# Strassen-type products of a hybrid attention and pooling layer: the rounded operand and its rest as one 512-column moving operand, and the spread of the norms by transposition

## The chip, the cores and the metric

The kernel runs on one core of a Trainium2 chip (trn2). The metric is the device time of one execution in microseconds, as the median of several runs. A core has a tensor engine (PE), a vector engine (DVE), a scalar engine (ACT), GpSimd (POOL) and SyncE (SP), which issues most DMAs. Each engine works through its own queue in order. They meet only at semaphores.

## The reference

One layer on x of 512 tokens x 2048 features, float32:

```python
hn   = RMSNorm(x) * pre_gain
q, k, v, g_a, u_b, g_b = split(hn @ w_in)          # 2048 -> 6 x 1024
z    = q k^T / sqrt(128)                           # 8 heads x 128, strictly causal
A    = sigmoid(z) * prod over s<j<t of (1 - sigmoid(z_tj))
y_a  = (A @ v) * silu(g_a)
y_b  = ((trailing mean of u_b over 2/4/8/16 tokens) - u_b) @ w_pool * pool_scale * silu(g_b)
x    = x + RMSNorm(concat(y_a, y_b) @ w_out) * post_gain
```

## The kernel before

**Arithmetic.** PE multiplies in a rounded 32-bit format (float32r). To keep float32 accuracy each operand is split into a rounded part (hi) and its rest (lo), and each product is three matmuls: hi x hi, hi x lo, lo x hi. They all stand in `three`, lines 1257 to 1259. A weight chunk `raw` of 128 x 1024 gets its `w_hi` on ACT (L470) and its `raw_lo` on DVE (L813).

**Values stage.** It takes 16 steps of K, each with 24 matmuls of 512 columns, and gives v for all tokens and heads in the 8 banks of PSUM. x comes transposed (`mix`); ACT makes `x_hi` (L451), DVE `x_lo` (L805). Beside it the norms are made. ACT squares x by rows (L475), DVE scales the sums (L904), POOL raises them to -1/2 (L1212). The result is one number per token, spread over the partitions; it must come to lie along the free dimension, on all 128 partitions (`rstd_rows`). Before, ACT issues a DMA into DRAM (L533) and another that broadcasts it back (L541). Then DVE multiplies `mix` by gain and `rstd_rows` (`hn_of`, L848) and forms the operands of the next stage.

**Product stage.** The other projections are 40 chunks of 128 output features. Two chunks form a unit, so there are 20 units. A unit is a 2 x 2 block product of Strassen's kind (Winograd's form): K is halved (8 tiles of 128 each) and the tokens are halved (256 each). Seven products replace eight: A11, R1, S2, S4, S3, A12, A22, the moving operands, made once for all units. Each lies in `a_hi` and `a_lo`. A product is 8 K tiles x 3 matmuls of 256 columns; stationary are `w_hi` or `raw_lo`. Products alternate between two PSUM banks, and later ones add onto what earlier ones left. ACT copies products 0, 1, 2 and 6 out (L567, L571, L573, L575), DVE combines products 3, 4 and 5 with these copies (L942, L944, L947). The weight sums that Strassen's form needs are made by DVE (`w_sum`, L828) and by accumulating DMAs of POOL.

Between the products of a unit PE does attention and pooling (`qk`, `suffix_sums`, `weighted_values`, `pool_tiles`), in a written-out order that repeats every five units. The softmax-like work on `tri` (128 x 1280) is on ACT, DVE and POOL.

**Output stage.** mix @ w_out, in 16 chunks of 128 x 2048 weights, split into hi and lo again. The split mix goes to the place of the first four operands in `a_hi` and `a_lo` (`mix_hi_of` L653, `mix_lo_of` L1042), three of the four weight slots to that of the last three (`o_hi_of` L665, `o_lo_of` L1051); the fourth is `o_hi3`/`o_lo3`.

What PE waits for before product p of unit u is in `product`: w_lo of this product; the copy or the combination of product p-2, whose bank it takes. ACT's w_hi of a product waits until the one three before is done, so both run at most two products ahead.

## Time and profile before

| | |
|---|---|
| median of 3 runs (lowest, highest) | 754.19 us (754.01, 757.17) |
| profiled execution: own time, span | 756.16 us, 754.4 us |
| PE busy, instructions | 736.1 us, 4912 matmuls |
| DVE busy, instructions | 481.5 us, 572 |
| ACT busy, instructions | 389.9 us, 530 |
| granted TensorE clock | 0.998 of full speed |
| HBM | 156 GB/s over the span |

The span goes from the first to the last instruction. Roughly, 0 to 100 us is the values stage, 101 to 567 the products with attention and pooling between them, 567 to 747 the output stage, and then the last rows are stored. In a row of the timeline the number in front is the start, the second the duration of one instruction (for x2 or x4, of all together); in brackets stands the idle time before it and what released it. Durations of matmuls overlap, so the pace is read from the starts.

### The profile page before, as it was taken

The numbers are of one execution on the slowest core, as the hardware profiler recorded it, in microseconds if no ns is written. First come the engines' busy times: TensorE is split into PE (matmuls) and PEld (weight loads), VectorE is DVE, ScalarE is ACT, GpSimd is POOL, SyncE is SP. The second block draws the span as 40 slices with busy tenths as digits, with TensorE's granted clock in tenths as the row PEclk, the third lists the DMA queues.
The fourth block names the chain that finished last, engine by engine and source line by source line (L and its number), as shares of the span: only waits on it lengthen the run. The fifth ranks groups of instructions, "written<-read, shape, count | busy, mean of one in ns | idle before, by whom it ended". The sixth has DMA issues, their size and how long they took to land.

```text
span 754.4 us, 11839 instructions
## 1 busy us (share of the span) xinstructions
PE 736.1 (98%) x4912; PEld 679.6 (90%) x4912; DVE 481.5 (64%) x572; ACT 389.9 (52%) x530; POOL 62.4 (8%) x85
## 2 busy tenths in 40 slices
PE   7999989999999999999999999999999999999996
PEld 5778879999999999999999999999998888888884
DVE  3379976767677767875786966776688532142333
ACT  4645466646656646665655566655569332132200
POOL 0000000110020110011100021020010000000000
PEclk9999999999999999999999999999999999999999
DMA  8944435666645756666555566556645613152242
GB/s 316 368 151 126 141 81 147 166 164 188 165 116 164 194 144 171 154 163 168 162 146 158 168 165 172 151 121 180 175 150 214 223 41 132 51 168 90 78 140 111
DMA packets 37060, 118.48 MB, mean 157 GB/s; under 512 B 4752, under 2 KB 5776, under 8 KB 36368
## 3 DMA queue, kind: packets, MB, share of 16 engines
q1 hardware_dynamic: 30288, 96.49, 37.1%
q0 software_dynamic: 5760, 20.97, 16.7%
q8 instruction: 39, 0.64, 0.3%
q10 hardware_dynamic: 960, 0.27, 0.2%
q14 instruction: 13, 0.11, 0.0%
HBM read 113.52 MB, written 4.20 MB: 156 GB/s over the span
## 4 chain that ended last, share of the span: by engine, by line
PE 83%; DVE 7%; DMA 4%; issue 3%; ACT 2%; SPq 1%; DVEq 0%; POOLq 0%; POOL 0%; ACTq 0%
PE ps L1257 27%; PE ps L1258 27%; PE ps L1259 27%; DMA mix<-xT 2%; PE ps L1348 1%; DVE mix L848 1%; DVE raw_lo L813 1%; PE ps L1346 1%; DMA rstd_rows<-rstd_dram 1%; DVE a_lo L881 1%; DVE a_lo L878 1%; DMA rstd_dram<-rstd_by_four 1%; ACT w_hi L470 1%; SPq L367 1%; DVE sum L853 0%
## 5 line engine op out<-in xcount | busy, mean ns | idle before, releaser
L1257 PE MATMUL ps<-a_hi,w_hi 128*128 128x256 f32 x1120 | 318.2, 284 | 3.5 <-ACT p_neg L571 1.3
L1258 PE MATMUL ps<-a_lo,w_hi 128*128 128x256 f32 x1120 | 316.9, 283 | 0.0
L1259 PE MATMUL ps<-a_hi,raw_lo 128*128 128x256 f32 x1120 | 316.8, 283 | 0.0
L813 DVE TENSOR_TENSOR raw_lo<-raw,w_hi 128x1024 fp32r<-128x1024 f32 x155 | 189.3, 1223 | 58.7 <-ACT w_hi L470 58.0
L1257 PEld LDWEIGHTS ps<-a_hi,w_hi 128*128 128x128 f32 x1120 | 214.8, 192 | 4.6 <-issue 3.0
L1258 PEld LDWEIGHTS ps<-a_lo,w_hi 128*128 128x128 f32 x1120 | 214.8, 192 | 0.4
L1259 PEld LDWEIGHTS ps<-a_hi,raw_lo 128*128 128x128 f32 x1120 | 214.8, 192 | 0.0
L470 ACT ACTIVATE w_hi<-raw 128x1024 fp32r<-128x1024 f32 x155 | 163.5, 1055 | 75.7 <-PE ps L1259 71.5
L1257 PE MATMUL ps<-a_hi 128*128 128x512 f32 x192 | 74.9, 390 | 0.0
L1258 PE MATMUL ps<-a_lo,a_hi 128*128 128x512 f32 x192 | 74.8, 390 | 0.0
L1259 PE MATMUL ps<-a_hi,a_lo 128*128 128x512 f32 x192 | 74.7, 389 | 0.0
L1228 POOL DMA_DIRECT2D raw<-w_heads x40 | 34.9, 871 | 322.4 <-DMA raw<-w_heads 286.1
L828 DVE TENSOR_TENSOR raw<-raw 128x1024 f32<-128x1024 f32 x40 | 48.8, 1220 | 10.5 <-DMA raw<-w_heads 9.5
L1051 DVE TENSOR_TENSOR a_lo<-raw,a_hi 128x1024 fp32r<-128x1024 f32 x24 | 28.5, 1229 | 39.1 <-ACT a_hi L665 39.1
L1257 PE MATMUL ps<-w_hi,x_hi 128*128 128x512 f32 x120 | 47.6, 397 | 2.4 <-DVE raw_lo L813 2.4
L665 ACT ACTIVATE a_hi<-raw 128x1024 fp32r<-128x1024 f32 x24 | 24.1, 1051 | 45.2 <-PE ps L1259 45.2
L1258 PE MATMUL ps<-raw_lo,x_hi 128*128 128x512 f32 x120 | 47.4, 395 | 0.0
L1259 PE MATMUL ps<-w_hi,x_lo 128*128 128x512 f32 x120 | 47.4, 395 | 0.0
L1259 PEld LDWEIGHTS ps<-a_hi,a_lo 128*128 128x128 f32 x192 | 36.1, 188 | 7.5
L1257 PEld LDWEIGHTS ps<-a_hi 128*128 128x128 f32 x192 | 36.1, 188 | 7.5
L1258 PEld LDWEIGHTS ps<-a_lo,a_hi 128*128 128x128 f32 x192 | 36.1, 188 | 7.4
L1218 POOL TENSOR_SCALAR_AFFINE_SELECT tri<-tri 128x256 f32<-128x256 f32 x32 | 24.0, 772 | 165.3 <-ACT tri L604 84.9
(135 smaller groups left out, 869.1 us busy)
## 6 DMA issues: line engine op xcount, KB each, us to landing
raw<-w_heads SPq DMA_DIRECT2D x100, 512.0 KB, 4.2
raw<-w_heads POOLq DMA_DIRECT2D x40, 512.0 KB, 6.4
raw<-w_out SPq DMA_DIRECT2D x32, 512.0 KB, 4.9
raw<-w_v SPq DMA_DIRECT2D x15, 512.0 KB, 11.7
mix<-xT SPq DMA_DIRECT2D x16, 256.0 KB, 10.5
x_rows<-x SPq DMA_DIRECT2D x4, 1024.0 KB, 13.3
raw<-x SPq DMA_DIRECT2D x8, 512.0 KB, 4.4
out<-mix SPq DMA_DIRECT2D x6, 512.0 KB, 2.7
```

What stands on the lines that cost most here:

```text
L367: sp.dma_start(raw_slot(raw, slot).rearrange("p (g c) -> p g c", g=2), v_weights(i)).then_inc(raw_loaded[slot], 16)
L470: act.activation(hi_slot(g), raw_slot(raw, slot), ACT.Copy).then_inc(w_hi_done, 1)
L665: act.activation(out_weights(a_hi, o_hi3, n % OUT_SLOTS)[:, b * QUARTER:(b + 1) * QUARTER], raw_slot(raw, half_slot(j)), ACT.Copy).then_in ...
L813: dve.tensor_tensor(raw_slot(raw_lo, slot), raw_slot(raw, slot), hi_slot(g).bitcast(F32), ALU.subtract).then_inc(w_split, 1)
L828: dve.tensor_tensor(raw_slot(raw, ROLE[u][p]), raw_slot(raw, ROLE[u][a]), raw_slot(raw, ROLE[u][b]), ALU.add).then_inc(w_summed, 1)
L848: dve.scalar_tensor_tensor(mix_tile(k), mix_tile(k), pre_gain_col[:, k:k + 1], rstd_rows[:, :], ALU.mult, ALU.mult).then_inc(hn_done, 1)
L1051: dve.tensor_tensor(out_weights(a_lo, o_lo3, n % OUT_SLOTS)[:, cols], raw_slot(raw, half_slot(j)), out_weights(a_hi, o_hi3, n % OUT_SLOTS) ...
L1218: pool.affine_select(out=sq, in_=sq, compare_op=ALU.is_gt, fill=0.0, base=0, pattern=[[0, 2], [1, P]], channel_multiplier=-1).then_inc(don ...
L1228: pool.dma_start(raw_slot(raw, slot), w_heads[unit_chunks(u)[1]][:, a:a + QUARTER], accum_op=ALU.add).then_inc(done, 16)
L1257: pe.matmul(dst, sta[0], mov[0], start=first, stop=False, skip_group_check=True)
L1258: pe.matmul(dst, sta[0], mov[1], start=False, stop=False, skip_group_check=True)
L1259: return pe.matmul(dst, sta[1], mov[0], start=False, stop=last, skip_group_check=True)
```

## The change

**Operands.** `a_hi` and `a_lo` become one tensor `a_ops`. A K tile of an operand is now 512 columns wide, 256 of hi and beside them 256 of lo. In a product, `w_hi` is multiplied with all 512 in one matmul, and `raw_lo` with the 256 of hi, into the second half of the bank. So a bank holds two partial results of 256 columns, which somebody must add.

**Drains.** ACT's copies of products 0, 1 and 2 and DVE's combinations of 3, 4 and 5 are 512 wide now. After each combination DVE folds: it adds the two halves (256 columns, out of SBUF). For product 6 ACT copies one half and DVE adds the other, a new instruction that stands at the start of the next unit in DVE's queue. PE waits for combinations, not for folds.

**Norms.** x is loaded by rows in natural order; the last of the four loads goes behind x and w_v of step 4, and the last square behind x_hi and w_hi of step 4. POOL's result is transposed by DVE in blocks of 32 x 32, and 16 small copies (8 on DVE, 8 on ACT) spread it over the partitions. The DMAs through DRAM are gone, and `rstd_col` needs none either.

**Output stage.** It computes the same; only the places of its operands within `a_ops` change.

```diff
             for i in (1, 2, 3): ...
-            square_of(3)
             x_hi_of(4)
             w_hi_of(4)
+            square_of(3)
             for i in range(2, V_STEPS):
-                if i == 3:
-                    act.wait_ge(rstd_ready, 1)
-                    act.dma_start(rstd_dram.rearrange("(p s) -> p s", s=TT),
-                                  rstd_by_four[:, :]).then_inc(rstd_sent, 16)
+                if i == 2:
+                    act.wait_ge(rstd_turned, 1)
+                    for to in (2, 3):
+                        for q in range(QUADRANTS):
+                            act.activation(rstd_part(to, q), turned_part(q), ACT.Copy).then_inc(rstd_spread, 1)
...
+            x_lo_of(4)
+            w_lo_of(4)
             dve.wait_ge(squared, TT)
             dve.tensor_scalar(ms_col[:, :], ss_col[:, :], 1.0 / D, EPS, ALU.mult,
                               ALU.add).then_inc(ms_ready, 1)
-            x_lo_of(4)
-            w_lo_of(4)
+            dve.wait_ge(rstd_ready, 1)
+            dve.transpose(sum1[:, 0:P].rearrange("p (s t) -> p s t", s=TT),
+                          rstd_col[:, :].unsqueeze(2).to_broadcast([P, TT, QUADRANT])).then_inc(rstd_turned, 1)
+            dve.wait_ge(rstd_turned, 1)
+            for to in (0, 1):
+                for q in range(QUADRANTS):
+                    dve.tensor_copy(rstd_part(to, q), turned_part(q)).then_inc(rstd_spread, 1)
...
             def combine(u, p):
...
                 if p == 3:
...
-                    dve.tensor_tensor(n2[:, 0:HALF], p2_neg[:, :], src, ALU.subtract).then_inc(combined, 1)
+                    dve.tensor_tensor(n2, p2_copy(u), src, ALU.subtract).then_inc(combined, 1)
+                    dve.wait_ge(combined, 4 * u + 1)
+                    dve.tensor_tensor(n2[:, 0:HALF], n2[:, 0:HALF], n2[:, HALF:SEQ],
+                                      ALU.add).then_inc(folded, 1)
...
-                    dve.tensor_tensor(n1[:, 0:HALF], p0_copy(u), src, ALU.add).then_inc(combined, 1)
+                    dve.wait_ge(copied, 4 * u + 4)
+                    dve.tensor_tensor(n1[:, HALF:SEQ], src[:, 0:HALF], n1[:, HALF:SEQ],
+                                      ALU.add).then_inc(combined, 1)
...
                 for p in range(PRODUCTS):
                     if p in (4, 5, 6):
                         combine(u, p - 1)
+                    if p == 0 and u > 0:
+                        combine(u - 1, 6)
...
             def product(u, p):
...
                 for k in range(KH):
-                    a = p * OPERAND + k * HALF
-                    mm = three(dst, both((hi, lo), k * P, (k + 1) * P), both((a_hi, a_lo), a, a + HALF),
-                               k == 0 and p in (0, 1, 5), k == KH - 1)
+                    a = p * OPERAND + k * SEQ
+                    w = slice(k * P, (k + 1) * P)
+                    pe.matmul(dst, hi[:, w], a_ops[:, a:a + SEQ], start=k == 0 and p in (0, 1, 5),
+                              stop=False, skip_group_check=True)
+                    mm = pe.matmul(dst[:, HALF:SEQ], lo[:, w], a_ops[:, a:a + HALF], start=False,
+                                   stop=k == KH - 1, skip_group_check=True)
```

On DVE in the values stage, from the scaling of the sums (`ms_col`) to the first `hn_of`, before:

```order
L904 TENSOR_SCALAR ms_col<-ss_col 128x4
L805 SCALAR_TENSOR_TENSOR x_lo<-mix,pre_gain_col,x_hi 128x512
L813 TENSOR_TENSOR raw_lo<-raw,w_hi 128x1024
L805 SCALAR_TENSOR_TENSOR x_lo<-mix,pre_gain_col,x_hi 128x512 x2
L813 TENSOR_TENSOR raw_lo<-raw,w_hi 128x1024
L805 SCALAR_TENSOR_TENSOR x_lo<-mix,pre_gain_col,x_hi 128x512
L813 TENSOR_TENSOR raw_lo<-raw,w_hi 128x1024
L848 SCALAR_TENSOR_TENSOR mix<-mix,pre_gain_col,rstd_rows 128x512 x4
```

The same place on DVE now:

```order
L822 SCALAR_TENSOR_TENSOR x_lo<-mix,pre_gain_col,x_hi 128x512
L830 TENSOR_TENSOR raw_lo<-raw,w_hi 128x1024
L924 TENSOR_SCALAR ms_col<-ss_col 128x4
L927 STREAM_TRANSPOSE sum<-rstd_col 128x128
L932 COPY rstd_rows<-sum 32x4x32 x8
L822 SCALAR_TENSOR_TENSOR x_lo<-mix,pre_gain_col,x_hi 128x512 x2
L830 TENSOR_TENSOR raw_lo<-raw,w_hi 128x1024
L822 SCALAR_TENSOR_TENSOR x_lo<-mix,pre_gain_col,x_hi 128x512
L830 TENSOR_TENSOR raw_lo<-raw,w_hi 128x1024
L867 SCALAR_TENSOR_TENSOR mix<-mix,pre_gain_col,rstd_rows 128x512 x4
```

x_lo and w_lo of step 4 stand ahead of the norms now, and nine instructions of the spread stand ahead of those of step 5.

On DVE in the last unit, from the combination of product 3 (`mix<-p_neg,ps`) over the softplus on `tri` to `gate_logsig` behind the loop, before:

```order
L942 TENSOR_TENSOR mix<-p_neg,ps 128x256
L961 SCALAR_TENSOR_TENSOR tri<-ps,tri 128x1280
L813 TENSOR_TENSOR raw_lo<-raw,w_hi 128x1024
L944 TENSOR_TENSOR mix<-p_neg,ps 128x256
L1051 TENSOR_TENSOR a_lo<-raw,a_hi 128x1024 x2
L947 TENSOR_TENSOR mix<-mix,ps 128x256
L966 TENSOR_TENSOR tri_lo<-tri,tri_hi 128x1280
L987 SCALAR_TENSOR_TENSOR gate_work<-mix,gate_work 128x512
```

The same place on DVE now:

```order
L968 TENSOR_TENSOR mix<-mix,ps 128x512
L970 TENSOR_TENSOR mix<-mix 128x256
L1001 SCALAR_TENSOR_TENSOR tri<-ps,tri 128x1280
L830 TENSOR_TENSOR raw_lo<-raw,w_hi 128x1024
L973 TENSOR_TENSOR p_neg<-p_neg,ps 128x512
L976 TENSOR_TENSOR mix<-p_neg 128x256
L1090 TENSOR_TENSOR a_ops<-raw,a_ops 128x1024 x2
L980 TENSOR_TENSOR mix<-mix,ps 128x512
L982 TENSOR_TENSOR mix<-mix 128x256
L1006 TENSOR_TENSOR tri_lo<-tri,tri_hi 128x1280
L986 TENSOR_TENSOR mix<-ps,mix 128x256
L1027 SCALAR_TENSOR_TENSOR gate_work<-mix,gate_work 128x512
```

Three folds came in behind the three combinations, and the combination of product 6 (L986) ahead of `gate_logsig`. In the other units it stands at the same point relative to the loop, ahead of the first `w_sum` of the next unit.

## Rows read from the trace of the kernel before

**Rows 1.** The page: busy us (share) xinstructions by engine; GB/s in 40 slices.
```profile
PE 736.1 (98%) x4912; PEld 679.6 (90%) x4912; DVE 481.5 (64%) x572; ACT 389.9 (52%) x530; POOL 62.4 (8%) x85
...
GB/s 316 368 151 126 141 81 147 166 164 188 165 116 164 194 144 171 154 163 168 162 146 158 168 165 172 151 121 180 175 150 214 223 41 132 51 168 90 78 140 111
```

**Rows 2.** Waits of PE: line, releaser: us in total, times, longest us.
```profile
PE ps L1257 <- DVE raw_lo L813: 2.4, 2, 1.8
PE ps L1257 <- ACT p_neg L571: 1.3, 1, 1.3
PE ps L1257 <- ACT mix L514: 1.1, 1, 1.1
PE ps L1257 <- ACT work L567: 1.1, 1, 1.1
```

**Rows 3.** Page, part 5: line, operation, shapes, xcount | busy, mean ns | idle.
```profile
L1257 PE MATMUL ps<-a_hi,w_hi 128*128 128x256 f32 x1120 | 318.2, 284 | 3.5 <-ACT p_neg L571 1.3
```

**Rows 4.** Timeline, PE in unit 8: start us, us, line, operation, xcount.
```profile
300.00 0.28 PE L1257 MATMUL ps<-a_hi,w_hi 128*128 128x256 f32 x1
...
302.88 0.28 PE L1257 MATMUL ps<-a_hi,w_hi 128*128 128x256 f32 x1
```

**Rows 5.** Timeline, PE in the output stage.
```profile
615.50 0.39 PE L1257 MATMUL ps<-a_hi 128*128 128x512 f32 x1
...
648.16 0.40 PE L1257 MATMUL ps<-o_hi,a_hi 128*128 128x512 f32 x1
...
659.13 0.40 PE L1259 MATMUL ps<-o_hi,a_lo 128*128 128x512 f32 x1
```

**Rows 6.** Timeline, POOL, ACT and DVE in the values stage.
```profile
28.15 1.02 POOL L1212 TENSOR_TENSOR rstd_by_four<-ms_col,neg_half 128x4 f32<-128x4 f32 x1 [26.36 <-DVE ms_col L904]
...
46.65 0.71 ACT L451 ACTIVATE x_hi<-mix,pre_gain_col 128x512 fp32r<-128x512 f32 x1
47.26 1.04 ACT L470 ACTIVATE w_hi<-raw 128x1024 fp32r<-128x1024 f32 x1
...
42.61 2.74 DVE L848 SCALAR_TENSOR_TENSOR mix<-mix,pre_gain_col,rstd_rows 128x512 f32<-128x512 f32 x4 [2.65 <-DMA rstd_rows<-rstd_dram]
...
48.34 1.23 DVE L813 TENSOR_TENSOR raw_lo<-raw,w_hi 128x1024 fp32r<-128x1024 f32 x1 [0.19 <-ACT w_hi L470]
```

**Rows 7.** Timeline, ACT and PE in unit 0.
```profile
111.28 1.26 ACT L514 ACTIVATE mix<-ps,rstd_col 128x512 f32<-128x512 f32 x2 [1.95 <-DVE a_lo L878]
...
112.97 0.36 PE L1257 MATMUL ps<-a_hi,w_hi 128*128 128x256 f32 x1 [1.33 <-ACT p_neg L571]
```

**Rows 8.** Groups by form on DVE: a 512-column instruction that reads PSUM.
```profile
L982 DVE TENSOR_TENSOR mix<-ps,mix 128x512 f32<-128x512 f32 x8 | 5.5, 691 | 0.7
```

**Rows 9.** Stretch 400:500: us, busy us (xinstructions) by engine, clock, DMA.
```profile
400.00:500.00 100.00, 100.00 (x809) 98.94 (x808) 74.69 (x84) 62.38 (x84) 12.02 (x14) 1.00 0.61 161
```

**Rows 10.** Timeline, DVE and PE at weighted_values of head 2.
```profile
274.59 1.49 DVE L971 TENSOR_TENSOR tri_lo<-tri,tri_hi 128x1280 fp32r<-128x1280 f32 x1
...
277.62 0.39 PE L1257 MATMUL ps<-tri_hi,v_hi 128*128 128x512 f32 x1
```

**Rows 11.** Timeline, DVE, ACT and PE in the last unit and after.
```profile
560.24 0.41 DVE L942 TENSOR_TENSOR mix<-p_neg,ps 128x256 f32<-128x256 f32 x1
...
561.97 1.21 DVE L813 TENSOR_TENSOR raw_lo<-raw,w_hi 128x1024 fp32r<-128x1024 f32 x1
...
568.10 0.69 DVE L987 SCALAR_TENSOR_TENSOR gate_work<-mix,gate_work 128x512 f32<-128x512 f32 x1 [0.36 <-ACT gate_work L631]
...
571.33 2.49 DVE L1042 TENSOR_TENSOR a_lo<-mix,a_hi 128x512 fp32r<-128x512 f32 x4
...
570.92 0.36 ACT L575 ACTIVATE mix<-ps 128x256 f32<-128x256 f32 x1
...
564.00 0.28 PE L1257 MATMUL ps<-a_hi,w_hi 128*128 128x256 f32 x1
...
575.17 0.39 PE L1257 MATMUL ps<-a_hi 128*128 128x512 f32 x1
```

More of the change, by code:

```diff
@@ L377, in _ @@
                 load_x_rows(i - 1)
+            load_x(4)
+            load_v(4)
             load_x_rows(3)
-            for i in (4, 5, 6):
+            for i in (5, 6):
                 load_x(i)
@@ L490, in a_hi_of @@
             def a_hi_of(q, op):
-                dst = operand(a_hi, op, q)
+                dst = operand(0, op, q)
                 if op in (A11, A12, A22):
@@ L495, in a_hi_of @@
                     half, tok = {A11: (0, 0), A12: (1, 0), A22: (1, 1)}[op]
-                    act.activation(split3(dst), pairs(mix, q, half, tok), ACT.Copy).then_inc(a_hi_done, 1)
+                    act.activation(dst, pairs(mix, q, half, tok), ACT.Copy).then_inc(a_hi_done, 1)
                     return
@@ L652, in mix_hi_of @@
                     act.wait_ge(pool_free, k - HEADS + 1)
[L653 removed]
+                act.activation(mix_part(k, 0), mix_tile(k), ACT.Copy).then_inc(mix_hi_done, 1)
             def o_hi_of(n):
@@ L1050, in o_lo_of @@
                     dve.wait_ge(o_hi_done, j + 1)
-                    dve.tensor_tensor(out_weights(a_lo, o_lo3, n % OUT_SLOTS)[:, cols],
+                    dve.tensor_tensor(out_weights(1, n % OUT_SLOTS)[:, cols],
                                       raw_slot(raw, half_slot(j)),
-                                      out_weights(a_hi, o_hi3, n % OUT_SLOTS)[:, cols].bitcast(F32),
+                                      out_weights(0, n % OUT_SLOTS)[:, cols].bitcast(F32),
                                       ALU.subtract).then_inc(o_split, 1)
@@ L1396, in _ @@
                             pool_tiles(2 * i + 1)
-            acts = (a_hi, a_lo)
             def rows_tile(dc, s, c):
                 slot = (KK * dc + c) % OUT_SLOTS
-                hi = out_weights(a_hi, o_hi3, slot)
-                lo = out_weights(a_lo, o_lo3, slot)
+                hi, lo = out_weights(0, slot), out_weights(1, slot)
                 for k in range(KC):
-                    a = (OUT_KK[c] * KC + k) * SEQ + s * P
-                    mm = three(rows_bank(dc, s), both(acts, a, a + P),
+                    tile = OUT_KK[c] * KC + k
+                    mm = three(rows_bank(dc, s), both((mix_part(tile, 0), mix_part(tile, 1)), s * P, (s + 1) * P),
                                both((hi, lo), k * BANK, (k + 1) * BANK),
```

149 lines of the change are left out of this document (81 added, 68 removed).

## The prediction

> **What bounds the kernel now.** I read the busy table first. The tensor engine (PE) is busy for 98% of the span, the vector engine (DVE) for 64%, the scalar engine (ACT) for 52% [rows 1]. The waits of PE come next: besides the first load there are five, worth 5.9 us of idle time, and they all lie in the first 115 us [rows 2]. From there to the end PE never waits. So time can only come from what PE does per instruction, from those early waits, or be lost where another engine becomes late.
>
> A busy row says nothing about pace, since matmuls overlap. The groups by form give the count: 1120 K tiles in the 140 products, three matmuls of 256 columns each [rows 3]. The starts give the pace. Between the two starts in [rows 4] lie 24 matmuls: 2.88 us / 24 = 120 ns, so 360 ns for a K tile, 403 us in all. That is over half of the span. The output stage shows 512 columns with new weights each time: 144 steps in 32.66 us = 226.8 ns where the moving operand lies in a_hi or a_lo, 47 steps in 10.97 us = 233.4 ns where it lies in o_hi3 or o_lo3 [rows 5].
>
> **The product's K tile.** Three matmuls of 256 columns become one of 512 (w_hi against a_hi and a_lo side by side) and one of 256 (raw_lo against a_hi). Columns stay at 768, weight loads go from three to two. Were time only columns, 512 would cost 2 x 120 = 240 ns and nothing would be won. The rows show 226.8 to 233.4, so about 7 to 13 ns belong to the instruction and not to its columns. The new pair then costs 226.8 + 120 = 347 ns or 233.4 + 120 = 353 ns. The moving operand of the products lies in a_ops, where a_hi was, which is the case of the first number; the stationary one is w_hi, which no 512 row has in that place. I take 348.5, nearer the first. Saving: 11.5 ns x 1120 = 12.9 us; ends 7.3 and 14.6 us, and 0 if the alternation of sizes costs what the merging gives.
>
> Here the Trainium skill speaks against the change (TensorE: Matmul & The Clock Gate, section Back-to-back issue gap): a warm matmul is spaced by its columns at 2.4 GHz plus about 2.5 ns, whatever its size. An estimate by that page is 2.5 x 1120 = 2.8 us saved. The trace does not agree with its sizes: 256 columns take 120 ns and not 109, 512 take 227 to 233 and not 216, at a granted clock of full speed.
>
> **The spread of the norms.** Now POOL's power ends at 28.15 + 1.02 = 29.17 us, and the first scaling of x by rstd_rows starts at 42.61 on DVE, because two DMAs through DRAM lie between [rows 6]. From there DVE works almost without a pause, and w_lo of value step 7 is ready only at 48.34 + 1.23 = 49.6; PE waits 1.8 us for it [rows 2, 6]. Its other wait on raw_lo, 0.6 us, is for step 4. A value step is 24 matmuls of about 233 ns, 5.6 us. So step 7 was due at 47.8, and steps 4 to 6 fill the time from 31.0 on. After the change, step by step:
> - The loads of x and w_v for step 4 pass the last megabyte of x_rows. DVE has w_lo of step 4 earlier and the 0.6 us wait goes: step 4 starts at 30.4.
> - 0.75 MB now go ahead of the last of x_rows, 2.0 us at 368 GB/s [rows 1]. The last square comes later by that and the power ends near 31.2.
> - DVE transposes (one instruction of 128 columns, then 8 copies of 128), ACT makes 8 more. No row has this shape. The nearest is a 256-column DVE instruction of 0.41 us [rows 11]; a shorter one should last less, and a queue of them starts faster than they last, so I take 0.2 us each, ends 0.1 and 0.41. Both engines are done near 33.3 (ends 32.5 and 35).
> - ACT's copies now stand ahead of x_hi(5), x_hi(6) and w_hi(5) in its queue. x_hi holds it for 0.61 us, w_hi lasts 1.04, w_lo after it 1.23 [rows 6]: w_lo of step 5 is ready near 36.9, and PE wants it at 36.0. A new wait of 0.9 us.
> - w_lo of step 6 follows within DVE's next 1.8 us, so the scaling starts near 38.6, 4 us earlier. w_lo of step 7 comes near 45.6 against a demand at 48.1, so the 1.8 us wait goes.
> Net so far: 0.6 + 1.8 - 0.9 = 1.5 us.
>
> DVE stays busy from here until the last a_lo, so its 4 us lead goes on to the first products. Three waits stand there: 1.1 for the value drain, 1.1 for the copy of product 0, 1.3 for the copy of product 1 [rows 2, 7]. The last is a chain: a_lo on DVE, two drains on ACT from 111.28, the copy, PE at 112.97 [rows 7]. With DVE 4 us earlier, that product starts near 109.4. The copies of 512 columns add 0.25 us to this chain. Product 4 starts about 3.5 us earlier than now; this 3.5 us contains the 1.5 above. Ends: 1 us (the small copies cost double and delay step 5 by 3 us) and 4.5 us.
>
> **The wider drains.** A DVE instruction on 512 columns out of PSUM takes 691 ns [rows 8], on 256 columns 0.41 us; ACT pays 0.36 us for 256 [rows 11] and 1.26 us for two drains of 512 [rows 7]. Per unit of seven products ACT gets three copies 0.25 us longer. DVE gets three combinations 0.27 us longer, three folds of 256 columns (0.35 us each) and a fourth combination of 0.35 us that waits for ACT's copy: some 2.3 us per 20 us. DVE has 75 us of work in 100 us there [rows 9], so it rises to about 87% and still fits. What hides it is PE's work on the other bank. The tightest recurring place that the longer drains touch is weighted_values: DVE's weights_lo ends at 274.59 + 1.49 = 276.08, PE needs it at 277.62 [rows 10], slack 1.5 us. ACT's wider copy takes 0.25 of it, faster products 0.2, about 1 us stays. A combination is now done one product less 0.7 us before PE needs its bank, 2.2 us; 0.3 to 0.5 of that goes. So I cost all of it at nothing in units 0 to 18. If that cover were gone, each unit would lose what DVE is behind.
>
> **The last unit.** Here DVE has the output operands to split as well, and does not idle. The combination of product 3 starts at 560.24 only, w_lo of product 6 ends at 561.97 + 1.21 = 563.2, and PE starts product 6 at 564.00 [rows 11]. After the change ACT's copies push by 0.25, combination and fold add 0.6, and the next combination (on which product 6 waits too) 0.3: ready at 564.8, wanted at 563.65. PE loses 1.2 us. The same once more at the handoff to the output stage: 0.4 us. Then the new combination of product 6 stands in DVE's queue ahead of gate_logsig. It waits for ACT's copy, which ends now at 571.3 (570.92 + 0.36) and then near 572.2, since the longer DVE chain delays POOL's mask and so ACT. Behind it are queued, as now from 568.10 to 571.33 + 2.49 = 573.82, 5.7 us of work ending with the mix operands that PE needs at 575.17 [rows 11]. From 572.6 that gives 578.0; PE, delayed by the above, wants it at 576.4. Wait 1.6 us. Sum 3.2 us lost; ends 0.5 and 5.
>
> **The sum**, against the profiled execution (span 754.4, own time 756.16): - 12.9 - 3.5 + 3.2 = - 13.2, span 741.2, own time 743.0. The median of before is 754.19, 2 us under that execution; the same step gives 741.0. I forecast 741.
>
> **Rivals.**
> - The pair costs what three cost (360 ns): the alternation breaks the overlap of loads and matmuls. For it: no row alternates 512 and 256. Against: the 226.8. Then 754.2 - 3.5 + 3.2 = 754. Chance 0.07.
> - Only a small part per instruction is saved. As a mechanism: the extra over columns in [rows 4, 5] (13 to 20 ns per matmul) goes with the columns read, and 2 to 3 ns with the instruction. Then 3 us are won and the time is 751. This is the rule of the Trainium skill's page named above. Chance 0.04.
> - Slower: DVE becomes the bound in the product loop. Place: w_lo in the iterations that now also hold combination and fold. It decides from the point at which DVE is behind by more than its slack of about 1.5 us; then each of 19 units loses about one w_lo (1.13 us), 21.5 us in all: 741 + 21.5 = 762. Against it speak the 75% of [rows 9]. Chance 0.05.
> - Better: the pair at 347 ns, early waits all gone (4.5), handoff at 0.5: 754.2 - 14.6 - 4.5 + 0.5 = 735.6. Chance 0.12.
> - The rest is worse than thought (pair 353, startup 1, handoff 5): 754.2 - 7.3 - 1 + 5 = 751, half of it under 750. Chance 0.08.
> - The forecast, 736 to 747: 0.64.
>
> **How the numbers follow.** What a measurement of this kernel can tell from no change is about 0.5%, 3.8 us: faster is under 750.4. Forecast, better and half of the last case give 0.80, and of the cases near 751 and of the slower one a part would still end under it: 0.86. Same 0.09, slower 0.05. The range 735 to 750 leaves out the two no-gain rivals and the slower one.
>
> **What would show it.** Starts of the two matmuls of a K tile: 227 to 233 ns and then 120 ns apart (right), 240 and 120 (wrong). The scaling of x starting at 38 to 39 us, a wait of about 1 us for w_lo of step 5. Product 4 starting near 112. No PE wait from there to the last unit; if there are waits on DVE there, the slower rival is at work. In the last unit waits on DVE of about 3 us in sum. A loop without waits and a time above 750 would say that the pair costs more than 357 ns.

## The result and the profile after

The changed kernel takes 749.34 us (median of 6 runs, 749.08 to 750.37), the kernel before 754.11 us on the same chip. The ratio is 0.994, 95% interval 0.993 to 0.995: 4.8 us won. The forecast was 741 us, 13.2 us won. The sign was right, the time lies in the range of 735 to 750, 0.7 us from its end, and the gain was overrated by a factor of nearly three. Of all executions used below one, the profiled one of e9_moved_64, ran at a granted clock of 0.825 and took 821.9 us; no time or row is taken from it.

The page of the changed kernel, busy time and the two groups of the product stage; they answer to [rows 1, 3].

```profile
span 747.4 us, 9753 instructions
...
PE 726.2 (97%) x3792; PEld 618.4 (83%) x3792; DVE 527.9 (71%) x661; ACT 406.0 (54%) x538; POOL 62.8 (8%) x85
...
L1361 PE MATMUL ps<-a_ops,w_hi 128*128 128x512 f32 x1120 | 397.9, 399 | 3.6 <-ACT p_neg L584 1.6
L1363 PE MATMUL ps<-a_ops,raw_lo 128*128 128x256 f32 x1120 | 314.2, 281 | 0.0
```

1120 matmuls of 512 and 1120 of 256 columns stand where 3360 of 256 stood. DVE rose from 481.5 to 527.9 us, 71%, and is still far from being the bound.

All waits of PE in the changed kernel, in the columns of [rows 2]:

```profile
PE ps L1316 <- ACT w_hi L538: 6.3, 1, 6.3
PE ps L1299 <- DVE raw_lo L830: 2.1, 2, 1.8
PE ps L1361 <- ACT p_neg L584: 1.6, 1, 1.6
PE ps L1361 <- ACT work L580: 1.4, 1, 1.4
PE ps L1299 <- DVE a_ops L1082: 1.1, 1, 1.1
PE ps L1361 <- DVE p_neg L973: 0.5, 1, 0.5
PE ps L1299 <- DVE mix L980: 0.3, 1, 0.3
```

The first is the first load. The next three lie before 111 us, the last three in the last unit and at the handoff to the output stage. Between 111 and 553 us PE waits for nobody.

A second execution of the kernel before was profiled too (`e1_before_again`), and it is the fairer basis, since it is nearer its median. The span by stages, in us, from the starts of PE's instructions (units 1 to 18 go from the first matmul of unit 1 to the first of unit 19; the recorded expectations call the same stretch units 1 to 19):

| | before, again (e1) | changed | difference |
|---|---|---|---|
| start to the first product | 100.54 | 98.67 | -1.87 |
| unit 0 | 23.12 | 23.22 | +0.10 |
| units 1 to 18 | 418.60 | 411.24 | -7.36 |
| unit 19 | 23.45 | 24.65 | +1.20 |
| output stage | 180.06 | 181.50 | +1.44 |
| from the start of the last matmul to the end | 7.47 | 8.12 | +0.65 |
| span | 753.2 | 747.4 | -5.8 |

The table says where the forecast went: units 1 to 18 gave 7.4 us where their share of the 12.9 was 11.6. The time up to unit 1 fell by 1.8 us, 0.4 of it by the pairs of unit 0, so 1.4 stand against a forecast of 3.5. The end took about what was forecast.

### The profile page after: what moved, and what is told of

Same layout as the page of the kernel before. It is cut to its first block, busy times and chain, and to the rows that moved or that the text cites. A ratio compares the mean times of both kernels' runs of the same rounds, so it can differ in the third digit from the quotient of the medians.

```text
span 747.4 us, 9753 instructions
## 1 busy us (share of the span) xinstructions
PE 726.2 (97%) x3792; PEld 618.4 (83%) x3792; DVE 527.9 (71%) x661; ACT 406.0 (54%) x538; POOL 62.8 (8%) x85
## 4 chain that ended last, share of the span: by engine, by line
PE 79%; DVE 9%; ACT 4%; issue 3%; DMA 2%; SPq 1%; POOL 0%; DVEq 0%; POOLq 0%; ACTq 0%
PE ps L1361 33%; PE ps L1363 17%; PE ps L1301 9%; PE ps L1300 9%; PE ps L1299 9%; DMA x_rows<-x 2%; DVE raw_lo L830 2%; DVE mix L867 1%; PE ps L1391 1%; PE ps L1389 1%; ACT w_hi L486 1%; DVE a_ops L899 1%; DVE a_ops L897 1%; DVE a_ops L1082 1%; SPq L381 0%
## 5 line engine op out<-in xcount | busy, mean ns | idle before, releaser
L1361 PE MATMUL ps<-a_ops,w_hi 128*128 128x512 f32 x1120 | 397.9, 399 | 3.6 <-ACT p_neg L584 1.6
L1363 PE MATMUL ps<-a_ops,raw_lo 128*128 128x256 f32 x1120 | 314.2, 281 | 0.0
L1361 PEld LDWEIGHTS ps<-a_ops,w_hi 128*128 128x128 f32 x1120 | 210.5, 188 | 55.8 <-DVE raw_lo L830 2.5
L1363 PEld LDWEIGHTS ps<-a_ops,raw_lo 128*128 128x128 f32 x1120 | 211.5, 189 | 0.3
L1299 PE MATMUL ps<-a_ops 128*128 128x512 f32 x192 | 75.0, 391 | 1.4 <-DVE a_ops L1082 1.1
L1300 PE MATMUL ps<-a_ops 128*128 128x512 f32 x192 | 74.8, 390 | 0.0
L1301 PE MATMUL ps<-a_ops 128*128 128x512 f32 x192 | 74.7, 389 | 0.0
L1090 DVE TENSOR_TENSOR a_ops<-raw,a_ops 128x1024 fp32r<-128x1024 f32 x24 | 28.3, 1219 | 37.8 <-ACT a_ops L682 37.8
L682 ACT ACTIVATE a_ops<-raw 128x1024 fp32r<-128x1024 f32 x24 | 24.0, 1050 | 43.9 <-PE ps L1301 42.8
L1299 PEld LDWEIGHTS ps<-a_ops 128*128 128x128 f32 x192 | 36.0, 188 | 9.5 <-issue 2.1
L1301 PEld LDWEIGHTS ps<-a_ops 128*128 128x128 f32 x192 | 36.0, 188 | 7.6
L1300 PEld LDWEIGHTS ps<-a_ops 128*128 128x128 f32 x192 | 36.0, 188 | 7.5
L1206 DVE TENSOR_TENSOR mix<-ps,post_gain_rows 128x512 f32<-128x512 f32 x16 | 11.0, 689 | 40.9 <-ACT gate_work L797 28.2
L797 ACT ACTIVATE gate_work<-ps 128x512 f32<-128x512 f32 x8 | 4.8, 598 | 49.1 <-PE ps L1301 49.1
```

The source lines that it names most:

```text
L682: act.activation(out_weights(0, n % OUT_SLOTS)[:, b * QUARTER:(b + 1) * QUARTER], raw_slot(raw, half_slot(j)), ACT.Copy).then_inc(o_hi_don ...
L1090: dve.tensor_tensor(out_weights(1, n % OUT_SLOTS)[:, cols], raw_slot(raw, half_slot(j)), out_weights(0, n % OUT_SLOTS)[:, cols].bitcast(F3 ...
L1299: pe.matmul(dst, sta[0], mov[0], start=first, stop=False, skip_group_check=True)
L1300: pe.matmul(dst, sta[0], mov[1], start=False, stop=False, skip_group_check=True)
L1301: return pe.matmul(dst, sta[1], mov[0], start=False, stop=last, skip_group_check=True)
L1361: pe.matmul(dst, hi[:, w], a_ops[:, a:a + SEQ], start=k == 0 and p in (0, 1, 5), stop=False, skip_group_check=True)
```

## The experiments

Three explanations were open at the outset: the pair is dearer than forecast in itself, or the small shift of the tiles that comes with the norms' edit makes it dearer, or the two edits get in each other's way at the start. The recorded expectations name theories A, B and so on anew for each run. Four kernels take the change apart.

### The parts alone

`e1_before_again` is the kernel before, unchanged.

> The kernel before, unchanged, for a second profile. The first profiled execution took 756.16 us against a median of 754.1. Theory A (the 2 us are a slow start of that one execution): the span is near 752.4, unit 0 ends about 2 us earlier than in the first profile, everything after it has the same length. Theory B (they lie elsewhere): the starts up to unit 1 (124.56 us) agree within 0.3 us.

Measured: 754.98 us, span 753.2, one run. PE waits for raw_lo once, for 1.2 us, and not twice, for 2.4 us in all [rows 2]. Unit 1 starts at 123.66 us, 0.9 us earlier, and units 1 to 18 take 418.60 us in both. So part of what theory A supposed is there, and 1.2 us of the execution on which the prediction's sum rests were waits at the start that another execution does not have.

`e2_pairs_only` is the changed kernel with the old norms:

```diff
+        rstd_by_four = sb("rstd_by_four", [P, TT])
...
-                    act.wait_ge(rstd_turned, 1)
-                    for to in (2, 3): ...                  # the copies
+                    act.dma_start(rstd_dram..., rstd_by_four[:, :])
```

> The change without its norms: pair of 512 and 256 columns, wide drains and folds, but the spread of the norms through DRAM as before. From the trace after: pair 353.9 instead of 360 ns, 0.41 us per unit, 8.2 us for 20 units, less 2.7 us of waits in the last unit. Theory A (the norms bring almost nothing): 749 to 750, a gain of 4.5 to 5.5. Theory B (the norms bring the 2.5 us that the two profiles show): 751 to 752, a gain of 2 to 3.

Measured: 748.5 us (747.89 to 750.51), ratio 0.9917 (0.990 to 0.993). That is better than both theories had it, and less than the changed kernel takes. Units 1 to 18 take 408.33 us, 2.9 us less than with both edits, though the products are the same instructions on operands at the same places. What lies elsewhere are the tiles behind `rstd_by_four`, those of attention and pooling among them.

`e3_norms_only` is the kernel before with the new norms, tiles kept in place:

```diff
-        rstd_by_four = sb("rstd_by_four", [P, TT])
+        sb("same_place", [P, TT])
```

> The norms by transposition alone, products as before; x_hi and its neighbours stay at the addresses of before. Theory A (before's profile was a slow start): gain 0 to 1 us, 753 to 754. Theory B: gain 2.5 us, 751.5. In both the first scaling of x starts near 39.7 us.

Measured: 752.19 us (751.11 to 752.73), ratio 0.9965 (0.995 to 0.998), between the two theories; units 1 to 18 in 418.60 us as before. The profiled execution is the fastest of the six. In it the first scaling of x starts at 37.86 us and not near 39.7, PE has no wait for w_lo, and unit 1 starts at 119.79 us, 3.9 us earlier than in e1. The last rows of x set this: the last square, on ACT, waits for their DMA and starts here at 26.25 us, in the changed kernel at 28.13.

```profile
26.25 1.92 ACT L483 ACTIVATE x_rows<-x_rows 128x2048 f32<-128x2048 f32 x1 [0.97 <-DMA x_rows<-x]
```

```profile
28.13 1.92 ACT L491 ACTIVATE x_rows<-x_rows 128x2048 f32<-128x2048 f32 x1 [1.37 <-DMA x_rows<-x]
```

So one profile tells what the norms win at the start only to within a microsecond or two; the medians say 2.2 us.

`e4_aligned_only` is the kernel before with a small unused tile that takes 32 bytes per partition, after which x_hi, tri, q, k and o_hi3 lie at multiples of 128 and not at 96 modulo 128. (Places are worked out from the order and sizes of the tiles in the kernel, each rounded up to 32 bytes; the traces do not print them.)

```diff
         rstd_by_four = sb("rstd_by_four", [P, TT])
+        sb("align_pad", [P, TT])
```

> The kernel before with 32 bytes of padding, which puts x_hi, x_lo, o_hi3 and what follows at multiples of 64 bytes, as the changed kernel does by dropping rstd_by_four. Theory A (the faster value steps after, 5.49 instead of 5.60 us, come from the address): value steps take 5.49 us here too. The time: since DVE's chain sets the start of products 2 and 3, PE's 1.5 us turn into longer waits there and the time is within 0.3 us of before. Rival: the steps keep 5.60 us and the faster ones came from something else in the change; or the 1.5 us show in full, 752.6.

Measured: 753.06 us (751.91 to 754.22), ratio 0.9977 (0.997 to 0.999). The output stage takes 178.58 and not 180.06 us: with o_hi3 as the moving operand it now runs at 226.5 ns a matmul and not 233.4 [rows 5]. A step of the values stage takes 5.44 us and not 5.60, but waits at the start take that back: the first product starts at 100.47 us, in e1 at 100.54. Units 1 to 18 take 418.46 us, in e1 418.60: the old products hardly change with these places.

So the pairs are worth 5.8 us, the norms 2.2, the places alone 1.3. The first two should give 8 together; the changed kernel gives 4.8. The change does one thing that neither e2 nor e3 does: without `rstd_by_four` everything behind it moves by 32 bytes.

### The places of the tiles

`e5_shift32` gives the 32 bytes back and `e6_shift64` twice as many; `e7_narrow_first` exchanges the two matmuls of a K tile.

```diff
         rstd_col = sb("rstd_col", [P, TT])
+        sb("pad", [P, 8])        # e5; 16 in e6
```

```diff
-                    pe.matmul(dst, hi[:, w], a_ops[:, a:a + SEQ], start=..., stop=False)
-                    mm = pe.matmul(dst[:, HALF:SEQ], lo[:, w], a_ops[:, a:a + HALF], ...)
+                    pe.matmul(dst[:, HALF:SEQ], lo[:, w], a_ops[:, a:a + HALF], start=..., stop=False)
+                    mm = pe.matmul(dst, hi[:, w], a_ops[:, a:a + SEQ], ...)
```

> The changed kernel with 32 unused bytes per partition ahead of ss_col, so that everything behind them (x_hi, x_lo, tri_hi, tri_lo, q, k, v_hi, work, gate_work, p1_neg) lies where it lay before and in the run with the pairs alone: at 32 modulo 64. a_ops, w_hi, raw, raw_lo do not move, and the instructions are the same. In the changed kernel a product of 8 K tiles takes 2.70 to 2.75 us nearly everywhere (pair 353.5 ns); in the pairs alone about 60% of the products take 2.66 us (pair 347 ns). Theory A (the place of the other tiles decides in which of two paces the products run): units 1 to 19 take 408.3 us in place of 411.2, the short pace shows in units 2, 3 and 5 to 8 as in the pairs alone, time 749.3 - 2.9 = 746.4. Rival B (the norms' edit is to blame, or which pace comes is chance from build to build): units 1 to 19 stay at 411 us, time 749.3. Rival C (the values stage loses what it had gained by the old places, 16 x 0.1 us): the loop gains 2.9 and 1.6 is lost, 748.0.

> The changed kernel with 64 unused bytes at the same place, so everything behind them stays at a multiple of 64 and moves from 64 to 0 modulo 128. Theory A with only 64 as its rule: loop as in the changed kernel, units 1 to 19 411.2 us, time 749.3. Theory A with 128 as its rule: o_hi3 as moving operand of the output stage paces 226.5 ns as in the aligned kernel before (o_hi3 at 0 modulo 128) and not 233.5 as in the changed one (64 modulo 128), which gives 1.3 us in the output stage, 748.0, and the loop may change its pace too. Rival B (chance): anything from 746 to 749.5 with no pattern by unit.

> The changed kernel with the two matmuls of a K tile exchanged: first raw_lo x 256 columns, then w_hi x 512. The bank, the drains and the sums are the same. If each matmul has a price of its own (512: 236, 256: 118), nothing changes: 749.3, the pair at 353 to 354 ns. If the long pace comes from which load stands behind which matmul, the pair changes: 347 ns would give units 1 to 19 in 405.5 us and 743.5; 360 ns would give 757.

Measured. The kernel before, run beside the three new ones, took 753.86 us. A product counts as short when its pairs, without the first, which other work ahead of it can stretch, are under 350 ns apart in the mean; no product lies between 347.8 and 352:

| | us | ratio | units 1 to 18 | products at the short pace | output stage |
|---|---|---|---|---|---|
| changed kernel | 749.34 | 0.994 (0.993 to 0.995) | 411.24 | 13 of 140 | 181.50 |
| pairs only | 748.5 | 0.992 (0.990 to 0.993) | 408.33 | 80 | 181.16 |
| e5_shift32 | 746.3 | 0.990 (0.988 to 0.991) | 408.17 | 82 | 181.49 |
| e6_shift64 | 746.3 | 0.990 (0.988 to 0.991) | 408.92 | 67 | 180.06 |
| e7_narrow_first | 747.39 | 0.991 (0.989 to 0.993) | 408.38 | 77 | 181.53 |

e5 comes out as its theory A to a tenth of a microsecond: with the tiles back at their places, 32 unused bytes win 3 us. In units 1 to 18 it has the short pace in the very 78 products in which the pairs alone have it, and e8 below, a third kernel with these places, has it there too. The sum of the parts holds again (5.8 + 2.2 = 8.0 against 7.6). That the norms' edit itself harms the pairs is refuted, and so is chance from build to build. Rival C is refuted too: the steps of the values stage do return from 5.49 to 5.60 us and the first product starts 1.5 us later than in the changed kernel, but PE's wait for the copy of product 0 shrinks from 1.4 to 0.2 us, and unit 1 starts only 0.4 us later.

In e6 theory A with 64 as its rule is refuted, since the loop is not at 411.2 us. With 128 as its rule it is right for the output stage, below, but the time is 746.3 and not 748.0, since the loop took a third pattern. In e7 none of the three times came: the pairs keep their two paces, in other products. So the places do not decide alone which pace comes; the order of the two matmuls does too.

What "pace" means is seen in the starts of the matmuls. PE in the changed kernel, near 300 us:

```profile
300.22 0.40 PE L1361 MATMUL ps<-a_ops,w_hi 128*128 128x512 f32 x1
300.45 0.28 PE L1363 MATMUL ps<-a_ops,raw_lo 128*128 128x256 f32 x1
300.57 0.40 PE L1361 MATMUL ps<-a_ops,w_hi 128*128 128x512 f32 x1
...
302.34 0.40 PE L1361 MATMUL ps<-a_ops,w_hi 128*128 128x512 f32 x1
```

From 300.22 to 302.34 are six pairs, 353 ns each. Within three pairs the 512 takes 232, 241 and 236 ns, over and over. And PE in e5_shift32, near 250 us:

```profile
249.81 0.39 PE L1362 MATMUL ps<-a_ops,w_hi 128*128 128x512 f32 x1
250.04 0.28 PE L1364 MATMUL ps<-a_ops,raw_lo 128*128 128x256 f32 x1
250.16 0.39 PE L1362 MATMUL ps<-a_ops,w_hi 128*128 128x512 f32 x1
...
251.54 0.39 PE L1362 MATMUL ps<-a_ops,w_hi 128*128 128x512 f32 x1
```

Five pairs in 1.73 us, 346 ns: 230 + 117 each time. (In 12 of the 13 short products of the changed kernel and 43 of the 67 of e6 a second form with the same mean stands, 231 + 113 and 233 + 117 in turn.) Behind the first pair a product is kept at one pace, and so are the next products until attention or pooling work, or a wait, comes between; behind it the pace may be the other. The pattern repeats with the period of five units. In e6 the output stage shows the other effect of places: with o_hi3, the moving operand, at 0 modulo 128 a matmul takes 226.6 ns, at 64 (changed kernel) and 96 (before, e5) 233.5. The values stage shows a third: there only the stationary operands, x_hi and x_lo, change their places with these edits, and yet a step takes 5.44 us at 0 modulo 128 (e4, e6, e10, e12), 5.49 at 64 (changed, e7) and 5.60 at 96 (all others read here).

### The order of work at both ends

`e8_moved_work` is e5 with work moved in three places. At the start:

```diff
-                if i == 2:
+                if i == 3:
                     act.wait_ge(rstd_turned, 1)
                     for to in (2, 3): ...       # now behind x_hi_of(i + 3) and w_hi_of(i + 2)
```

At the end:

```diff
             h = HEADS - 1
-            combine(LAST_UNIT, 6)
             gate_logsig_of(h, 0)
             o_lo_of(1)
+            combine(LAST_UNIT, 6)
```

and, third, in the last unit wp_lo goes behind w_lo. `e9_moved_64` has 64 bytes of padding, `e10_narrow_moved_64` the 256 columns first as well.

> As e5_shift32, with two instructions orders mended. At the start ACT's 8 small copies stand behind w_hi of step 5 and not ahead of x_hi of step 5: PE's wait of 1.8 us for w_lo of step 5 goes, the first scaling of x starts at about 38.0 us (39.7 in the changed kernel). At the end DVE's new combination of product 6 stands behind gate_logsig and the split of the second output chunk, and in the last unit wp_lo behind w_lo. If the waits of PE there (0.31 + 0.68 + 0.47 + 1.28 = 2.7 us) come from this order, they go, and with the start 4.4 us are won against e5_shift32: 742.0. Rival: DVE has no room in the last unit, whatever the order; the waits move and only the 1.7 us of the start are won: 744.7.

> As e8_moved_work, with 64 unused bytes and not 32, so that the tiles behind them lie at 0 modulo 128. If the places act alike with and without the moved work: output stage 1.4 us shorter (o_hi3 as moving operand 226.5 ns and not 233.5), units 1 to 19 in 408.9 us and not 408.2, in sum 742.3 - 1.4 + 0.7 = 741.6. Rival: the loop's pace comes out at random again (408.2 to 411.3), 741 to 744.

> As e9_moved_64, with the 256-column matmul first in each K tile. In e7_narrow_first this exchange gave 408.4 us for units 1 to 19 at places where the other order took 411.2, with the same two paces of 347 and 353.5 ns, only entered at other units. If the exchange only changes in which units the short pace is entered, the loop here lies between 405.5 (all short) and 411.5 (all long) and the time between 738.5 and 744.5; I expect 408.5 and 741.2. If the exchange favours the short pace as such, it is 406 or less, and under 739.

Measured: e8 742.27 us (741.85 to 743.09), ratio 0.984 (0.983 to 0.986); e9 741.6 (741.04 to 742.06), ratio 0.983 (0.981 to 0.984); e10 741.42 (740.82 to 743.24), ratio 0.983 (0.981 to 0.985), with 85 products at the short pace, units 1 to 18 in 408.60 and the output stage in 178.64 us. All three came within 0.3 us of what was expected, and beat the changed kernel by 7 to 8 us. Whether the stages of e9 did what was expected of them no trace shows.

The start in the changed kernel: POOL's power, DVE's transposition and copies, ACT's copies and what is queued behind them, PE's wait for w_lo of step 5, the scaling of x.

```profile
30.42 1.02 POOL L1254 TENSOR_TENSOR rstd_col<-ms_col,neg_half 128x4 f32<-128x4 f32 x1 [28.63 <-DVE ms_col L924]
```

```profile
31.47 0.31 DVE L927 STREAM_TRANSPOSE sum<-rstd_col 128x128 f32<-128x128 f32 x1 [1.14 <-POOL rstd_col L1254]
31.82 1.96 DVE L932 COPY rstd_rows<-sum 32x128 f32<-32x128 f32 x8
...
36.79 1.23 DVE L830 TENSOR_TENSOR raw_lo<-raw,w_hi 128x1024 fp32r<-128x1024 f32 x1
...
39.73 2.73 DVE L867 SCALAR_TENSOR_TENSOR mix<-mix,pre_gain_col,rstd_rows 128x512 f32<-128x512 f32 x4
```

```profile
31.82 2.63 ACT L553 ACTIVATE rstd_rows<-sum 32x128 f32<-32x128 f32 x8 [1.68 <-DVE sum L927]
34.48 1.34 ACT L467 ACTIVATE x_hi<-mix,pre_gain_col 128x512 fp32r<-128x512 f32 x2
35.72 1.04 ACT L486 ACTIVATE w_hi<-raw 128x1024 fp32r<-128x1024 f32 x1
```

```profile
38.16 0.47 PE L1299 MATMUL ps<-w_hi,x_hi 128*128 128x512 f32 x1 [1.84 <-DVE raw_lo L830]
```

Eight copies take DVE 1.96 us (245 ns each) and ACT 2.63 us (329 ns each). ACT waits 1.68 us for the transposition first, with x_hi of step 5 queued behind; w_lo of step 5 is ready at 36.79 + 1.23 = 38.02 and PE loses 1.84 us. In e8 the same places are:

```profile
30.21 1.50 ACT L468 ACTIVATE x_hi<-mix,pre_gain_col 128x512 fp32r<-128x512 f32 x2
31.62 1.04 ACT L487 ACTIVATE w_hi<-raw 128x1024 fp32r<-128x1024 f32 x1
32.69 2.63 ACT L558 ACTIVATE rstd_rows<-sum 32x128 f32<-32x128 f32 x8
```

```profile
35.31 1.22 DVE L831 TENSOR_TENSOR raw_lo<-raw,w_hi 128x1024 fp32r<-128x1024 f32 x1
...
38.25 2.73 DVE L868 SCALAR_TENSOR_TENSOR mix<-mix,pre_gain_col,rstd_rows 128x512 f32<-128x512 f32 x4
```

x_hi and w_hi fill the time in which ACT had waited. The scaling starts at 38.25 (in e5 at 40.09, with the last square within 0.2 us of the same start), and PE's wait for raw_lo, 2.25 us in e5, shrinks to 0.2 us.

The end, DVE in the changed kernel:

```profile
547.36 0.43 DVE L1068 TENSOR_TENSOR wp_lo<-wp_raw,wp_hi 128x256 fp32r<-128x256 f32 x1 [3.13 <-ACT wp_hi L661]
547.70 1.22 DVE L830 TENSOR_TENSOR raw_lo<-raw,w_hi 128x1024 fp32r<-128x1024 f32 x1
...
552.50 1.22 DVE L830 TENSOR_TENSOR raw_lo<-raw,w_hi 128x1024 fp32r<-128x1024 f32 x1
553.63 0.68 DVE L973 TENSOR_TENSOR p_neg<-p_neg,ps 128x512 f32<-128x512 f32 x1
...
561.15 0.42 DVE L986 TENSOR_TENSOR mix<-ps,mix 128x256 f32<-128x256 f32 x1 [1.66 <-ACT mix L591]
561.49 0.68 DVE L1027 SCALAR_TENSOR_TENSOR gate_work<-mix,gate_work 128x512 f32<-128x512 f32 x1
...
564.36 2.90 DVE L1082 TENSOR_TENSOR a_ops<-mix,a_ops 128x512 fp32r<-128x512 f32 x4
```

and PE there:

```profile
554.46 0.47 PE L1361 MATMUL ps<-a_ops,w_hi 128*128 128x512 f32 x1 [0.52 <-DVE p_neg L973]
557.78 0.47 PE L1299 MATMUL ps<-a_ops 128*128 128x512 f32 x1 [0.31 <-DVE mix L980]
567.41 0.47 PE L1299 MATMUL ps<-a_ops 128*128 128x512 f32 x1 [1.12 <-DVE a_ops L1082]
```

wp_lo waits 3.13 us for ACT with the next w_lo behind it, and DVE is late from there on. The new combination (L986) waits 1.66 us for ACT's copy at 560.34, with gate_logsig, o_lo and the mix operands behind it, and PE waits 1.12 us for these. In e8:

```profile
541.35 1.22 DVE L831 TENSOR_TENSOR raw_lo<-raw,w_hi 128x1024 fp32r<-128x1024 f32 x1 [1.70 <-ACT w_hi L487]
542.82 0.43 DVE L1069 TENSOR_TENSOR wp_lo<-wp_raw,wp_hi 128x256 fp32r<-128x256 f32 x1 [0.24 <-ACT wp_hi L662]
...
556.61 0.41 DVE L987 TENSOR_TENSOR mix<-ps,mix 128x256 f32<-128x256 f32 x1
556.95 2.48 DVE L1083 TENSOR_TENSOR a_ops<-mix,a_ops 128x512 fp32r<-128x512 f32 x4
```

Now w_lo stands ahead of wp_lo and starts 12.8 us after the unit's first product (528.6) and not 14.6 (533.1), the combination finds its copy ready with gate_logsig and o_lo done before it, the mix operands start 28.4 us into the unit and not 31.2, and of PE's waits at the end only 0.3 us is left: unit 19 takes 23.53 us and the output stage 180.15, together 2.8 us less than in e5. The rival (DVE has no room there) is refuted. The two moves at the end were made together, and what each is worth is not shown.

### What switches the pace

`e11_extra_columns` and `e13_wide_switched` (both from e8) and `e12_narrow_switched` (from e10) put one useless matmul ahead of some products; in e11:

```diff
                 dst = product_bank(g)
+                extra = EXTRA.get((u, p), 0)
+                if extra:
+                    pe.matmul(dst[:, 0:extra], hi[:, 0:P], a_ops[:, p * OPERAND:p * OPERAND + extra],
+                              start=True, stop=False, skip_group_check=True)
```

> e8_moved_work with one useless matmul of N columns ahead of eight products (its sums are cleared by the product's first matmul, start=True): ahead of product 5 of units 3, 8, 13, 18 with N = 128, 136, 144, 152, and ahead of product 1 of units 4, 9, 14, 19 with N = 160, 168, 176, 184. It shifts the moment at which the product starts by 3.3 ns from one N to the next. In e8_moved_work all eight products and those behind them run at the long pace (353.5 ns a pair). Theory phase: which pace comes is decided by the moment of the start relative to something that ticks, so at some N the product behind runs at 347 ns and keeps it to the end of the unit, at other N it doesn't. Rival position: the pace hangs on where the instructions lie in PE's queue or on what stands ahead of them; then all eight act alike, all long or all short. Time: 742.3 + 8 x 0.065 = 742.8, less 0.05 us for each product that turns short.

> e10_narrow_moved_64 with one useless matmul of 128 columns ahead of product 0 of unit 1 and product 1 of units 5, 10 and 15 (cleared by the product's first matmul). In e10 these four stand at the start of runs of 8, 14, 14 and 14 products at the long pace (353.5 ns a pair, 236 + 118). Theory switch: one more matmul there turns them to the short pace, for at least the products up to the next attention work; if it holds through, 50 products x 8 x 6.5 ns = 2.6 us are won and 4 x 0.115 paid: units 1 to 19 in 406.3 and not 408.6, time 739.2. Rival (chance of the place): products behind it stay at the long pace, time 741.4 + 0.5 = 741.9.

> e8_moved_work with one useless matmul of 128 columns ahead of product 5 of units 3, 8, 13 and 18 alone. In e11 products 5 and 6 and product 0 of the next unit turned to the short pace behind it, and then a second one turned product 1 back. Theory switch: without the second, product 1 of units 4, 9, 14, 19 stays at the short pace too, and what follows depends on the pooling work behind it. Gain at least 4 x (4 x 8 x 6.5 ns - 0.115 us) = 0.4 us, at most 4 x (10 x 8 x 6.5 ns - 0.115) = 1.6 us: 740.7 to 741.9. Rival: 742.3 or more.

e11 took 743.0 us, one run. PE in e11 around the extra matmul ahead of product 5 of unit 3, which stood in a run at the long pace:

```profile
181.75 0.22 PE L1365 MATMUL ps<-a_ops,w_hi 128*128 128x128 f32 x1
181.81 0.45 PE L1370 MATMUL ps<-a_ops,w_hi 128*128 128x512 f32 x1
182.09 0.28 PE L1372 MATMUL ps<-a_ops,raw_lo 128*128 128x256 f32 x1
182.21 0.39 PE L1370 MATMUL ps<-a_ops,w_hi 128*128 128x512 f32 x1
182.44 0.28 PE L1372 MATMUL ps<-a_ops,raw_lo 128*128 128x256 f32 x1
```

From the extra matmul to the start of the 256 are 0.34 us, and then the short pace holds: 0.23 and 0.12. So at all four places with 128 to 152 columns. At the four others, with 160 to 184 columns, the run ahead was at the short pace (an effect of the first four), and behind the extra matmul it was at the long one. The width had no part in it: extra matmul and 512 together take 341 to 346 ns for every width from 128 to 184; what a narrower one saves, the 512 behind it takes longer. Neither theory had this right. The shift of 3.3 ns that "phase" needed never reached the product, so that theory wasn't tested; "position" asked for one answer at all eight places, and they gave two.

In e12 the extra matmul switched unit 1 from long to short, where it stood right between products, and at units 5, 10 and 15, where it stood behind attention work, it did nothing: still 236 ns. Behind unit 1 the rest of unit 2 and the first three products of unit 3, short in e10, came out long. The time is 741.76 us (741.11 to 742.83), and units 1 to 18 take 409.70 against 408.60: the forecast of 739.2 was wrong. The extra matmuls take some 0.5 us of it and a wait for q_lo in unit 4, which e10 does not have, 0.8. e13 behaved as forecast for the products behind (products 5 and 6 and five of the next unit at the short pace), but measured 741.75 us (741.08 to 743.0) against 742.27: half a microsecond, not told apart from nothing. Units 1 to 18 took 408.30 us against 408.17, though 103 and not 78 of their products are short, which is worth 25 x 52 ns = 1.3 us. The four extra matmuls take 0.5 of that, and a wait of PE in unit 1 that e8 does not have takes 0.8:

```profile
PE ps L1303 <- DVE q_lo L998: 0.8, 1, 0.8
```

So inside the loop, too, a faster PE can now meet a wait for DVE.

What stands: the pace is kept within an unbroken row of pairs, and may change behind other matmuls. An odd matmul right between two pairs changed it in all 13 cases (8 in e11, 1 in e12, 4 in e13), to the short one from the long and back; behind attention work it did so in none of 3. What DVE and ACT do at the moment does not set it: in units 1 to 18 the 512s of the changed kernel have a median of 236 ns beside DVE's w_lo (352 of them), beside an idle DVE (116) and beside an idle ACT (298); those of the pairs alone have 230 in all three cases. What makes the two paces, and which of the shifted tiles counts, is open.

## Why the prediction was wrong, step by step

- **The pair: the step that failed.** It took 348.5 ns a pair, near the sum of the output stage's 226.8 and the product's 120. Measured are 353.8 ns in the mean over units 1 to 18 (882 pairs), and the saving was 7.4 us there where 11.6 was forecast. The sign that it named, 227 to 233 ns and then 120, did not come: the 512 takes 236 ns in the mean and the 256 117. The mechanism was right: a pair costs less than three matmuls. The low end of 347 ns exists, in 82 of 140 products of e5, though in only 13 here. That it fits to the nanosecond is luck, since its parts there are 230 and 117 and not 226.8 and 120. What the argument lacked is that a pace read in one stage had two values (226.8 and 233.4 in [rows 5]) whose cause was not known. I tied them to the operand and took the nearer; the change moved tiles by 32 bytes, and that was not priced at all. It costs 3 us of the loop (411.24 against 408.33 in e2 and 408.17 in e5). The other 1.2 us of the 4.2 are missing in e5 as well, where the mean pair takes 350.5 ns.
- **The Trainium skill's rule** (TensorE: Matmul & The Clock Gate, section Back-to-back issue gap) makes the spacing the columns at 2.4 GHz plus about 2.5 ns. The Trainium skill's page gives this for an isolated matmul, and about 131 ns for 512 columns in a sustained stream with weight loads. The traces agree with neither: they show 112 to 120 ns for 256 columns and 224 to 241 for 512, at full granted clock. The saving estimated by this rule, 2.8 us, is too small (7.4 in 18 units alone); the forecast's was too large.
- **The basis.** The prediction carried the step from one execution, 2 us above its median, over to the median, and so counted that execution's own waits (1.2 us of raw_lo) as something to be won. Its first scaling of x starts at 42.61 us, that of e1 at 41.69: 0.9 us of the 4 us of lead that was forecast for the new norms are this.
- **The spread of the norms.** Right in kind: the last square later (28.13 us, in e1 25.44), the step 4 wait gone, a new wait for w_lo of step 5. Wrong in size: POOL's power ends at 31.44 us and not 31.2, the copies cost 0.245 and 0.33 us and not 0.2, so that ACT is done at 34.45 and not 33.3; the new wait is 1.84 and not 0.9 us, and the scaling starts at 39.73 and not 38.6. So the lead of DVE is 1.96 us against e1. In e3 it was 3.8 us, with an earlier last square and no wait for step 5: how much of the forecast comes hangs on when the last rows of x land. Alone the norms win 2.2 us in the median; 3.5 was forecast. Moving ACT's copies brings 1.8 (unit 1 starts at 120.40 us in e8 and at 122.25 in e5).
- **The first unit.** It came out 0.1 us longer. The wider drains were costed at 0.25 us there, in the chain to product 3 [rows 7]. PE now waits 1.6 us for the copy of product 1 and 1.4 for that of product 0, together 0.5 more than in e1, and the 0.4 us that its pairs save are gone. The chain itself shows the price: product 3 starts 70.4 us after DVE's first scaling of x in all four traces with the old drains, and 70.8 in all ten with the wide ones. So the wide drains cost 0.4 us here, and otherwise the start of the scaling is what counts.
- **Wide drains in the loop at nothing: right.** No wait from 111 to 553 us, and the folds' 425 ns lie beside PE's work. The rival with DVE as the bound did not come.
- **The last unit and the handoff: right.** Forecast 1.2 + 0.4 + 1.6 = 3.2 us lost; unit 19 lost 1.2 on top of the 0.4 that its pairs save, the output stage 1.44, 3.0 us in sum, at the places named. The wait behind the new combination is the 1.12 us of L1082.
- **The end of the span** costs 0.65 us more behind the last matmul, in every kernel with pairs and in none without. The instructions there last as long as before and start at the same distances, up to the issue of the last store. That store lands 2.81 us after its issue and not 2.16; why is open.

Together, in spans against e1: forecast 13.2 us, measured 5.8. The difference of 7.4 is, to 0.15, 4.7 for the pairs (12.9 less 7.4 and twice 0.4), 2.1 for the start and the first unit (3.5 less 1.4), 0.65 behind the last matmul, and -0.2 in the last unit and the handoff. The last 1.0 us to the medians' 4.8 is that e1's execution, too, lay 0.9 us above the median of 754.1.

## What to carry to other kernels

Before an edit that adds or removes a small tile is timed, pad it so that all others keep their places, or try a few paddings: here 32 bytes were worth 3 us, over half the measured gain, and hid the value of both edits. When a matmul of one shape shows two paces in a trace, carry both into the sum, and do not choose between them by a cause that no run has tested. When a new instruction waits for another engine, put behind it only what nobody needs soon: three moves without any change in work won 4 us here (746.3 to 742.27). And read the start from more than one execution: two of the same kernel differed by 0.9 us there.
